# The first two output panels behind a norm, worked abreast k-tile by k-tile

## The reference

```
h = h + 0.5 * rmsnorm(swiglu(rmsnorm(h, n[0]), ffn1_wi, ffn1_wo), n[1])
h = h + rmsnorm(hybrid_mixer(rmsnorm(h, n[2]), w_in, ...), n[3])
h = h + 0.5 * rmsnorm(swiglu(rmsnorm(h, n[4]), ffn2_wi, ffn2_wo), n[5])
```

## Time and profile before

| | |
|---|---|
| median of 3 runs | 1102.33 us |
| the profiled execution's own time | 1100.94 us |
| its span, first to last instruction | 1099.1 us |
| mean granted TensorE clock | 0.968 |
| matmuls on PE | 8206 |
| busy share DVE, ACT, POOL | 58%, 43%, 66% |
| share of the chain of waits: PE, DVE, ACT, POOL | 80%, 9%, 4%, 3% |

### The profile page before, as it was taken

One profiled execution on the slowest core, in us unless ns is written; L12 is line 12 of the kernel. 1 busy time (PEld: TensorE's weight loads), 2 busy tenths in 40 slices (PEclk: granted clock), 3 DMA queues, 4 the chain that ended last, 5 costly groups with the idle time before them and its releaser, 6 DMA issues.

```text
span 1099.1 us, 21438 instructions
## 1 busy us (share of the span) xinstructions
PE 1025.7 (93%) x8206; PEld 1000.1 (91%) x8206; DVE 638.8 (58%) x1028; ACT 478.0 (43%) x706; POOL 726.6 (66%) x327
## 2 busy tenths in 40 slices
PE   4799999998989999998989999989999979999996
PEld 4699999998989999997888888989999969999995
DVE  6333995445855555345794653537556666656454
ACT  5344223445354444434546523433225455445431
POOL 3785655555848787996467723556538829889993
PEclk9899999999999999998999889989999989999998
DMA  7454334442636655565344213433335626555661
GB/s 260 134 175 152 116 116 117 134 134 76 193 104 185 179 166 183 162 191 151 112 138 135 59 40 95 135 97 119 100 91 145 208 70 190 180 184 183 180 194 55
DMA packets 47865, 154.89 MB, mean 141 GB/s; under 512 B 5980, under 2 KB 11108, under 8 KB 47604
## 3 DMA queue, kind: packets, MB, share of 16 engines
q1 hardware_dynamic: 45648, 151.31, 45.1%
q10 hardware_dynamic: 2152, 2.65, 0.7%
HBM read 151.85 MB, written 2.10 MB: 140 GB/s over the span
## 4 chain that ended last, share of the span: by engine, by line
PE 80%; DVE 9%; ACT 4%; issue 3%; POOL 3%; DMA 0%; DVEq 0%; SPq 0%; ACTq 0%; POOLq 0%
PE panel L1492 63%; PE panel L1536 4%; PE aux L1603 2%; POOL wlo L569 2%; PE aux L1791 1%; DVE qkv L1218 1%; DVE qkv L1222 1%; DVE qkv L1227 1%; PE aux L1521 1%; PE aux L1828 1%; PE aux L1867 1%; ACT whi L650 1%; PE aux L1876 1%; PE aux L1838 1%; PE aux L1544 1%
## 5 line engine op out<-in xcount | busy, mean ns | idle before, releaser
L569 POOL TENSOR_TENSOR wlo<-raw,whi 128x1024 fp32r<-128x1024 f32 x284 | 700.7, 2486 | 344.8 <-ACT whi L650 344.7
L1492 PE MATMUL panel<-xh,whi 128*128 128x256 f32 (+1 forms) x1504 | 442.5, 294 | 16.1 <-DVE xl L959 10.0
L1492 PE MATMUL panel<-xh,wlo 128*128 128x256 f32 (+1 forms) x1504 | 430.9, 287 | 0.0
L1492 PE MATMUL panel<-xl,whi 128*128 128x256 f32 (+1 forms) x1504 | 430.5, 286 | 0.0
L650 ACT ACTIVATE whi<-raw 128x1024 fp32r<-128x1024 f32 x284 | 294.2, 1052 | 188.1 <-PE panel L1492 153.6
L1492 PEld LDWEIGHTS panel<-xh,whi 128*128 128x128 f32 x1504 | 287.9, 191 | 20.7 <-issue 11.8
L1492 PEld LDWEIGHTS panel<-xl,whi 128*128 128x128 f32 x1504 | 286.9, 191 | 1.6
L1492 PEld LDWEIGHTS panel<-xh,wlo 128*128 128x128 f32 x1504 | 287.7, 191 | 0.0
L1492 PE MATMUL panel<-hh,whi 128*128 128x272 f32 (+1 forms) x352 | 100.1, 284 | 0.0
L1492 PE MATMUL panel<-hh,wlo 128*128 128x272 f32 (+1 forms) x352 | 99.9, 284 | 0.0
L1492 PE MATMUL panel<-hl,whi 128*128 128x272 f32 (+1 forms) x352 | 99.8, 284 | 0.0
(11 more groups left out here) (293 smaller groups left out, 1593.0 us busy)
## 6 DMA issues: line engine op xcount, KB each, us to landing
raw<-in_panels SPq DMA_DIRECT2D x236, 512.0 KB, 3.5
raw<-in_down SPq DMA_DIRECT2D x32, 448.0 KB, 3.3
raw<-in_down SPq DMA_DIRECT2D x16, 512.0 KB, 3.5
memx<-in_mem SPq DMA_DIRECT2D x1, 1024.0 KB, 5.1
h<-in_x SPq DMA_DIRECT2D x1, 1024.0 KB, 8.3
spill<-h ACTq DMA_DIRECT2D x1, 1024.0 KB, 4.7
h<-spill ACTq DMA_DIRECT2D x1, 1024.0 KB, 7.7
out<-h SPq DMA_DIRECT2D x2, 512.0 KB, 2.9
```

Source lines behind the costliest of these rows:

```text
L569: nc.gpsimd.tensor_tensor(wlo[:, slot, :], raw[:, slot, :], whi[:, slot, :].bitcast(f32), ALU.subtract).then_inc(lo_ready, 1)
L1492: ins = M(bank[:, 0:w], wt[:, slot, P * t:P * t + P], x[:, kk, c0:c0 + w], start=first and m == 0 and n == 0, stop=last and m == len(pairs ...
```

## The change

`first_output` becomes `first_outputs` and takes a list of outputs. For each k-tile it multiplies for all of them and then adds the squares. The first output is passed at its last k-tile, the second right after. Both feed-forward blocks call it with panels 0 and 1, and the mixer with qkv 0 and qkv 1; the separate runs of panel 1 go. Nothing changes on the other engines.

```diff
+ABREAST = 2
@@
-            def first_output(o, p, w, n):
+            def first_outputs(outs, w, n):
 
                 bank, use = aux("stat", n)
-                open_output(o, p)
+                for o, p in outs:
+                    open_output(o, p)
                 aux_open(use)
                 for kk in range(KT):
                     pe.wait_ge(split_low, 8 * SPLIT[n] + kk + 1)
-                    ins = products(pb[o % 4], p % RING, [(kk, kk)], xh, xl, 0, w, kk == 0, kk == KT - 1)
+                    for o, p in outs:
+                        ins = products(pb[o % 4], p % RING, [(kk, kk)], xh, xl, 0, w, kk == 0, kk == KT - 1)
+                        if kk == KT - 1:
+                            ins.then_inc(passed, 1)
                     pe.wait_ge(squared, 8 * SPLIT[n] + kk + 1)
                     total = M(bank[:, 0:w], ones[:], sq[:, kk, 0:w], start=kk == 0, stop=kk == KT - 1)
-                ins.then_inc(passed, 1)
                 total.then_inc(aux_full, 1)
@@
-                first_output(first_o, first_p, w, norm)
-                for n in range(1, 4):
+                first_outputs([(first_o + n, first_p + n) for n in range(ABREAST)], w, norm)
+                for n in range(ABREAST, 4):
                     output(first_o + n, first_p + n, xh, xl, w)
@@
                 if step == ("qkv", 0):
-                    first_output(o, p, LEN, 5)
-                elif kind in ("qkv", "fourier_in", "sconv"):
+                    first_outputs([MIX_OUT[("qkv", n)][0:2] for n in range(ABREAST)], LEN, 5)
+                elif kind in ("qkv", "fourier_in", "sconv") and not (kind == "qkv" and i < ABREAST):
                     output(o, p, xh, xl, LEN)
```

## The result

The changed kernel takes 1112.59 us (median of 4 runs, 1111.84 to 1114.6), the kernel before, run beside it, 1102.24 us (4 runs, 1101.52 to 1103.56). The ratio is 1.0097, interval 1.0082 to 1.0111: slower by 1%, 10.3 us, where 10.2 was forecast. The profiled execution took 1112.62 us (span 1110.8, mean granted clock 0.961, before 0.968).

What follows compares the result with a forecast made beforehand. PE was taken as the bound, busy 1025.7 of 1099.1 us. Direct gain 0, stalls 3.0 + 2.85, mixer 1.9 and clock 2.4 sum to 10.15, added to 1102.33: 1112.5 us, range 1107 to 1116.5.

Steps and rivals of the forecast that it cites:

- Direct gain 0: All three norms: PE never waits between k-tiles, so the second panel has no idle time to fill; 0 us.
- One sign of being wrong: Mixer: PE's stage from first product to end of panel 1 shorter than 12.3 us would disprove the forecast.
- Stall at panel 3: Feed-forward blocks: late root delays panel 3's split, so PE waits once in each; 3.0 and 2.85 us, never given back.
- The sum ends one panel later: All three norms: last pass of the sum of squares comes behind both panels; 3.04 us at 272 columns, 2.85 at 256.
- The clock: Feed-forward blocks: PE's clock falls behind each new stall, 1.5 us each, four in five; 2.4 us, bounds 0 and 3.1.
- The mixer: Mixer's start: tile 1's pre is 1.9 us late and the delay is carried on; 1.9 us, bounds 0.5 and 3.0.
- the short end: Mixer: tile 1's L1218 gets in ahead of POOL, one tap instead of two is held, ba is 0.5 us late.
- rival 2: More than forecast: both falls, mixer's long end 3.0, a third fall as the ba wait reaches 4 us; 1115.8, chance 0.09.
- Rival 4: Mixer and second feed-forward block: PE starts norms at high clock, second panel fills 1.6 us in each; 1099.1, chance 0.05.
- The row at 576.12: Kernel before: clock didn't fall after a similar PE wait ending at 576.12; a 272-column panel took 3.12 us.

Runs made afterwards that it cites:

- feed-forward alone: Two panels abreast only in the two feed-forward blocks, mixer as in the kernel before: 1110.18 us, ratio 1.0068.
- mixer alone: Two panels abreast only in the mixer, feed-forward blocks as in the kernel before: 1105.95 us, ratio 1.0030.
- experiment 5: Changed kernel with panel 3's high part made ahead of each norm and POOL held back (gated) until all eight xl are made: 1106.0 us, ratio 1.0033.
- experiments 7 and 8: 7: feed-forward blocks only, second panel abreast for k-tiles 0 to 3, 1103.89 us, ratio 1.0017. 8: changed kernel with three panels abreast everywhere, 1123.55 us, ratio 1.0188.
- experiments 1 and 2: The kernels feed-forward alone (1110.18 us) and mixer alone (1105.95 us), in this order.
- experiment 3: Changed kernel with panel 3 split ahead of each norm, POOL not held back: 1109.61 us, ratio 1.0068.
- its control: Kernel before, one panel at a time, with panel 3 split early and POOL held back: 1102.72 us, ratio 0.9997.
- experiment 9: Kernel before with products of ones with ones filling PE's waits ahead of the norms (warm), nothing else changed: 1099.81 us, ratio 0.9977.
- 11: Kernel before, one panel at a time, warm, with panel 3 split early and POOL held back: 1097.34 us, ratio 0.9963.
- 12: Kernel before, warm, panel 3 split early with POOL held back, two panels abreast in the second feed-forward block only: 1098.08 us, ratio 0.9958.

## Why the prediction came out right

By its steps:

- *Direct gain 0: right.* Waits for xl unchanged. One sign of being wrong did come, a stretch from the mixer's first product to the end of panel 1 shorter than 12.3 us: it was 11.57. But nothing was filled. With the mixer as before and the same short low stretch, feed-forward alone needs 8.61 + 3.04 = 11.65, and mixer alone, with the long one, 12.32.
- *Stall at panel 3: right.* 2.81 us for the 3.0 taken, 2.99 - 0.19 = 2.80 for 2.85; never given back; removed by experiment 5, scaled by experiments 7 and 8.
- *The sum ends one panel later: right.* 2.99 in the first block. In this pair of traces it is 2.28 for 3.04 in the mixer, because the low level at the stage's start lasted less long: three k-tiles' sums ran at it before (0.91, 0.91, 0.88), and in the changed kernel not quite two (0.91, 0.72). Like with like it is 3.0 (9.29 to 12.32, 8.61 to 11.57). In the second block it is 2.27 for 2.85; there the kernels without the change lie between 8.72 and 9.16 among themselves, and the rest isn't explained.
- *The clock: right, and better than its odds.* I put four in five on each fall; both came, and after three panels both came again. The terms with the stalls were forecast at 3.0 + 2.85 + 2.4 = 8.25; the feed-forward part alone measured 7.5 by the ratio, 4.4 + 3.8 = 8.2 in the trace.
- *The mixer: the path right, the term wrong.* The first `pre` 3.0 and tile 1's 1.8 us late are as worked out, and so is the short end, with one tap held: +0.5 was forecast for it, 0.7 to 0.8 measured by experiments 1 and 2. The term taken was another one, the 1.9 by which the `pre` is late, for which PE doesn't wait. What it left out is the clock behind the longer wait, 1.81 us instead of 1.05: 4.73 - 3.24 = 1.5 us on panel 2. That fall was in rival 2 alone, tied there to a wait of 4 us. Together that is 2.3 of the 3.3 us of experiment 2. The rest is PE's work at the low level too, since the mixer's idle time didn't grow, but where it falls isn't settled: a second fall near 604 is in the changed kernel, in the mixer-only one and in experiment 3; the gated kernel has none there and a mixer just as long (379.7 us), with a fall behind the wait that ends at 579.56, behind which the clock holds in its control (576.42). The mixer's length also differs by several us between warm kernels that lack the change there (377.8 in experiment 9, 372.5 in 11, 375.5 in 12), so a single trace can't split it.
- *Rival 4, the faster case:* its mechanism is true and its size too, 1.7 us in each of two stages for the 1.6 it named. Its condition, a high clock at the first tiles, isn't met in this kernel. It left out that PE, ahead of time, pays at the next wait.

The total hit closer than its terms, and that is luck: 0.75 too much in the feed-forward blocks and 1.4 too little in the mixer partly cancel. The row at 576.12, with which the prediction argued that the clock can hold behind such a wait, is no safe example: behind the same wait the clock falls in ten of the fourteen traces (see the last section).

The rule of the Trainium skill that the prediction used (SBUF — State Buffer, Who interferes with whom) is borne out by experiments 3 and 5: the same two DVE operations took 1.45 us beside a started wlo and 0.88 without it. The lateness of `ba` in the mixer was, as by that rule, the short end and not a middle.

## What to carry to other kernels

Before moving work ahead of a reduction, look up who reads the reduction's result on an in-order engine and what is queued behind that reader: here everything that ACT had to split for later panels moved with the sum, and PE's slack there was zero. When PE is the bound, work added beside a wait gains only if PE is the one that waits; if its own low clock makes it late, filler products ahead of it gain more than reordering does. Price a wait of a few us on PE above its own length, for the clock behind it (here 2.8 us of wait cost 4.4 and 3.8), and count the small waits that grow, whether their feeder is later or PE sooner. Before a difference of a us or two between two traces is explained, look whether the low clock lay alike in both; a kernel with the change in one stage only gives the pair that tells.

## What the runs showed that was not expected

- The granted clock fell behind quite short waits in an otherwise busy stretch. All six traces with the panels abreast in the mixer have PE wait 1.80 or 1.81 us for `ba`, and the clock falls behind it in each; the eight others have 0.52 to 1.06 us there and no fall. At panel 3 it fell behind 2.81, 2.99 and 5.8 us and held behind 1.31 and 1.56. A fall cost 1.5 to 1.8 us of PE time. The Trainium skill (TensorE: Matmul & The Clock Gate, What's actually happening) has it that idle time brings the low clock back; the runs agree.
- The length of the wait alone doesn't decide. The wait that ends at 576.12 in the kernel before, 2.32 us, is in all fourteen traces (2.29 to 2.32 us); within 2 us behind it the clock falls in ten of them, the changed kernel and feed-forward alone among them, and not in four. Stretches of PE behind it, in the kernel before and in the changed one, where it ends at 581.22:

```profile
576.10:580.00 3.90, 3.88 (x32) 1.00 0.61 146
```
```profile
581.20:585.00 3.80, 3.78 (x19) 0.55 0.47 147
```

- Some 46 extra products of ones, none of which anyone reads, make the kernel 0.23% faster, and 0.37% with the early, gated split (the two intervals overlap).
- A split moved to where its engine is idle isn't free: the wlo beside DVE's norm work cost 2.1 us of the median (1.0019), the same split held back by one wait cost nothing (0.9997).
